# First-layer expert loop of a two-layer diffusion backbone: a third class of experts, four in three units

## The reference, cut to what matters

```python
D_MODEL, SEQ, CTX_LEN, DEPTH = 1024, 256, 256, 2
N_EXPERTS, TOP_K, EXPERT_HIDDEN = 64, 8, 128

def moe_ffn(h, rw, rb, w1, w3, w2, sw1, sw3, sw2):
    scores = jax.nn.sigmoid((h @ rw).astype(F32))
    ...
    _, eidx = lax.top_k(jnp.where(emask, sel, -jnp.inf), TOP_K)
    ...
    a = jnp.einsum('td,edh->teh', h, w1)
    b = jnp.einsum('td,edh->teh', h, w3)
    act = (jax.nn.silu(a) * b * gate[..., None])
    routed = jnp.einsum('teh,ehd->td', act, w2)
    shared = (jax.nn.silu(h @ sw1) * (h @ sw3)) @ sw2
    return (routed + shared)
```

## Time and profile before

| | us |
|---|---|
| median of three runs | 1427.9 (1424.88 to 1430.07) |
| the profiled execution's own time | 1431.2 |
| its span | 1429.1, mean granted clock 0.953 |
| TensorE (PE) busy | 1285.2 (90% of the span) |
| its weight loads (PEld) | 705.7 |
| VectorE (DVE) busy | 544.0 (38%) |
| ScalarE (ACT) busy | 293.5 (21%) |
| GpSimd (POOL) busy | 301.1 (21%) |
| DMA | 373.30 MB, mean 261 GB/s |
| chain that ended last | PE 41%, SyncE's queue 12%, DMA 8%, DVE 4% |

### The profile page before, as it was taken

How to read it: one execution, slowest core, us unless ns; L and a number is a source line. 1 busy time by engine, 2 the same in 40 slices (tenths; PEclk the granted TensorE clock), 3 DMA queues, 4 the chain that set the end, 5 groups by cost and what they waited for, 6 DMA issues and landing times.

```text
span 1429.1 us, 19065 instructions
## 1 busy us (share of the span) xinstructions
PE 1285.2 (90%) x6356; PEld 705.7 (49%) x6357; DVE 544.0 (38%) x1327; ACT 293.5 (21%) x715; POOL 301.1 (21%) x394
## 2 busy tenths in 40 slices
PE   4999998999968999989898969899987799999993
PEld 1443454444534666655565624475544354545441
DVE  5303533554665222223232207455456521211124
ACT  0100114233111222222221211212611111111110
POOL 1001004334123233333332300101710411111110
PEclk9999999999989999999999989999997899999997
DMA  9875309653355999999999379341322999999960
GB/s 334 328 283 191 142 0 267 238 204 119 140 191 211 332 382 377 363 375 370 383 378 390 119 299 364 125 155 25 94 104 83 399 397 392 404 408 398 404 250 31
DMA packets 113083, 373.30 MB, mean 261 GB/s; under 512 B 17978, under 2 KB 24380, under 8 KB 104792
## 3 DMA queue, kind: packets, MB, share of 16 engines
q1 hardware_dynamic: 89112, 313.50, 58.4%
q0 software_dynamic: 23008, 55.40, 10.6%
q10 hardware_dynamic: 864, 3.15, 0.6%
HBM read 368.77 MB, written 30.47 MB: 279 GB/s over the span
## 4 chain that ended last, share of the span: by engine, by line
PE 41%; SPq 12%; DMA 8%; DVE 4%; issue 3%; ACT 1%; POOL 0%; POOLq 0%; DVEq 0%; ACTq 0%
PE bank L1335 11%; SPq L647 10%; PE bank L1357 6%; PE bank L1367 5%; PE bank L943 3%; PE bank L1323 3%; DMA qkv<-in_exp_w 2%; PE bank L1145 2%; PE bank L951 2%; DMA weights<-in_exp_w 2%; DMA probs_T<-in_exp_w 2%; PE bank L1036 1%; PE bank L1026 1%; SPq L778 1%; PE bank L1188 1%
## 5 line engine op out<-in xcount | busy, mean ns | idle before, releaser
L1335 PE MATMUL bank<-weights,b_qk 128*64 128x256 f32 (+2 forms) x1040 | 160.8, 386 | 1.8 <-DVE b_qk L2295 1.5
L1335 PEld LDWEIGHTS bank<-weights,b_qk 128*64 128x64 f32 (+2 forms) x1040 | 110.7, 147 | 62.3 <-issue 34.6
L2301 DVE TENSOR_TENSOR expert_act<-silu_a,bank 128x128 f32<-128x128 f32 x76 | 21.9, 288 | 312.6 <-ACT silu_a L1658 312.6
L1367 PE MATMUL bank<-tokens_h,a_k 128*128 128x512 f32 x208 | 103.5, 622 | 0.0
L2532 POOL DMA_INDIRECT shift_scale_gate_norm<-scratch_h,gather_index x82 | 85.1, 1038 | 70.6 <-POOL gather_index L2529 68.4
L1357 PE MATMUL bank<-weights,expert_act_T 128*64 128x512 f32 (+2 forms) x260 | 91.9, 619 | 8.6 <-DMA weights<-in_exp_w 4.1
L1335 PE MATMUL bank<-features_h,b_qk 128*32 128x256 f32 (+2 forms) x512 | 95.2, 381 | 0.4
L1323 PE MATMUL bank<-tab,shift_scale_gate_norm 128*128 128x128 f32 x624 | 83.0, 276 | 8.4 <-DMA shift_scale_gate_norm<-scratch_h,gather_index 8.4
L1145 PE MATMUL bank<-weights,features_h 128*128 128x512 f32 x192 | 85.9, 602 | 1.3 <-ACT features_h L1445 0.7
L1658 ACT ACTIVATE silu_a<-bank 128x128 f32<-128x128 f32 x76 | 21.1, 278 | 314.7 <-PE bank L1335 314.7
L1323 PEld LDWEIGHTS bank<-tab,shift_scale_gate_norm 128*128 128x128 f32 x624 | 75.9, 191 | 17.6 <-issue 16.9
(11 more groups left out here) (360 smaller groups left out, 1960.4 us busy)
## 6 DMA issues: line engine op xcount, KB each, us to landing
weights<-in_exp_w SPq DMA_DIRECT2D x195, 512.0 KB, 12.1
features_h<-in_exp_w SPq DMA_DIRECT2D x64, 512.0 KB, 11.1
qkv<-in_exp_w SPq DMA_DIRECT2D x64, 512.0 KB, 15.8
shift_scale_gate_norm<-in_ada_w SPq DMA_DIRECT2D x24, 1024.0 KB, 8.8
a_q<-in_exp_w SPq DMA_DIRECT2D x32, 512.0 KB, 13.1
weights<-in_w_in SPq DMA_DIRECT2D x6, 2048.0 KB
shift_scale_gate_norm<-scratch_mod POOLq DMA_DIRECT2D x16, 512.0 KB, 8.7
c_padded<-in_ada_w SPq DMA_DIRECT2D x8, 1024.0 KB, 6.0
```

The costliest lines, as they stand in the source:

```text
L1335: mm = pe.matmul(ab[r, 0:2 * HIDDEN].rearrange("p (m h) -> p m h", m=2), XGT[:, u.slot() % 2, k, r], expert_w13(slot)[:, :, k, :], start=k ...
L1367: mm = pe.matmul(ACC[g][h][:, :], GROW[:, u.slot() % 2, g * P:(g + 1) * P], YSB[:, u.slot() % 2, h * HALF:(h + 1) * HALF], start=False, st ...
```

## The change

The classes become a table. In the first layer, the 24 experts of ranks 30 to 53 get 96 slot rows each instead of a unit of 128 each; four of them fill three units. The last ten experts keep a unit each. A middle expert of such a group has its 96 rows as strips of 64 and 32, which may lie in different units, so its weights are used by two units. Six groups make 18 units where there were 24, so the first layer has 44 units instead of 50, and `BLOCKS` there is 79 instead of 85. A group's three units run directly after one another. A load into a ring slot waits for the last unit that uses the expert that was there. The second layer keeps its units; its routing arithmetic is now written in the general form. `SHARE` of the first layer, the rows in which slots are counted, becomes 32.

```diff
@@ -46,12 +46,25 @@
 TILES = 4
 STREAMS = ((0, 1), (2, 3))
 FULL = ((0, 1, 2, 3), (2, 3))
-QUADS = (0, 8)
-PAIRS = (15, 14)
-SINGLES = tuple(EXPERTS - 4 * q - 2 * p for q, p in zip(QUADS, PAIRS))
-UNITS = tuple(q + p + f for q, p, f in zip(QUADS, PAIRS, SINGLES))
+QUAD = (tuple((e, slice(32 * e, 32 * e + 32)) for e in range(4)),)
+PAIR = (tuple((e, slice(64 * e, 64 * e + 64)) for e in range(2)),)
+FOUR_IN_THREE = (((0, slice(0, 64)), (0, slice(64, 96)), (1, slice(96, 128))),
+                 ((1, slice(0, 64)), (2, slice(64, 128))),
+                 ((2, slice(0, 32)), (3, slice(32, 64)), (3, slice(64, 128))))
+SINGLE = (((0, slice(0, P)),),)
+CLASSES = (((15, PAIR, 2), (6, FOUR_IN_THREE, 3), (10, SINGLE, 4)),
+           ((8, QUAD, 1), (14, PAIR, 2), (4, SINGLE, 4)))
+
+
+def experts_of(shape):
+
+    return 1 + max(e for unit in shape for e, _ in unit)
+
+
+UNITS = tuple(sum(n * len(shape) for n, shape, _ in classes) for classes in CLASSES)
+BOUNDS = tuple((c[0][0] * experts_of(c[0][1]), c[0][0] * experts_of(c[0][1]) + c[1][0] * experts_of(c[1][1])) for c in CLASSES)
 ALWAYS = (1, 0)
-SHARE = (64, 32)
+SHARE = (32, 32)
 UNROLL = 4
 RING = 3
 MASKED = -1e30
@@ -84,22 +97,27 @@
 
 def sequence(l):
 
-    held = SINGLES[l] - UNROLL if l < DEPTH - 1 else SINGLES[l]
-    kinds = [[QUADS[l], 4, 0, 0], [PAIRS[l], 2, QUADS[l], 4 * QUADS[l]],
-             [held, 1, QUADS[l] + PAIRS[l], 4 * QUADS[l] + 2 * PAIRS[l]]]
-    every, order = sum(k[0] for k in kinds), []
+    classes, held = CLASSES[l], UNROLL if l < DEPTH - 1 else 0
+    many = [n for n, _, _ in classes]
+    many[2] -= held
+    every, order = sum(many), []
     for n in range(every):
-        late = [((n + 1) * k[0] / every - order.count(i), i) for i, k in enumerate(kinds)]
...
+        late = [((n + 1) * k / every - order.count(i), i) for i, k in enumerate(many)]
         order.append(max(late)[1])
-    order += [2] * (SINGLES[l] - held)
-    seq, x, done = [], 0, [0, 0, 0]
+    order += [2] * held
+    column = [0, classes[0][0] * len(classes[0][1])]
+    column.append(column[1] + classes[1][0] * len(classes[1][1]))
+    where = [0, *BOUNDS[l]]
+    seq, x = [], 0
     for i in order:
-        _, many, column, where = kinds[i]
-        seq.append((column + done[i], [(x + j, where + many * done[i] + j) for j in range(many)]))
-        done[i] += 1
-        x += many
+        shape = classes[i][1]
+        for unit in shape:
+            seq.append((column[i], [(x + e, where[i] + e, r) for e, r in unit]))
+            column[i] += 1
+        x += experts_of(shape)
+        where[i] += experts_of(shape)
     for n in range(ALWAYS[l]):
-        seq.append((UNITS[l] + n, [(x + n, EXPERTS + n)]))
+        seq.append((UNITS[l] + n, [(x + n, EXPERTS + n, slice(0, P))]))
     return seq
...
-STRIPS = {n: tuple(slice(i * P // n, (i + 1) * P // n) for i in range(n)) for n in (1, 2, 4)}
...
 
                 def products(u, experts):
 
-                    rows = STRIPS[len(experts)]
-                    for slot, fills in experts:
+                    for slot, fills, _ in experts:
                         pe.wait_ge(L[f"w13_in{slot}"], fills * 32)
                     pe.wait_ge(L["xT_scalar"], u.n(1))
                     pe.wait_ge(L["xT_vector"], u.n(1))
                     for k in range(KD):
-                        for (slot, _), r in zip(experts, rows):
+                        for slot, _, r in experts:
                             mm = pe.matmul(ab[r, 0:2 * HIDDEN].rearrange("p (m h) -> p m h", m=2),
                                            XGT[:, u.slot() % 2, k, r], expert_w13(slot)[:, :, k, :],
...
-                    rows = STRIPS[len(experts)]
                     if h == 0:
                         pe.wait_ge(L["actT"], u.n(1))
...
-                    for (slot, _), r in zip(experts, rows):
+                    for slot, _, r in experts:
                         mm = pe.matmul(yp[h][r, :], ACTT[:, r], expert_w2(slot)[:, h * HALF:(h + 1) * HALF],
                                        start=True, stop=True)
                     mm.then_inc(L["y_ps"], 1)
...
-                    was, experts = (experts if n else None), [(x % ring_n, x // ring_n + 1) for x, _ in listed]
+                    was, experts = (experts if n else None), [(x % ring_n, x // ring_n + 1, r) for x, _, r in listed]
                     products(u, experts)
...
-                two, four = 4 * QUADS[l], 4 * QUADS[l] + 2 * PAIRS[l]
+                one, (two, four) = CLASSES[l][0][2], BOUNDS[l]
+                more_two, more_four = CLASSES[l][1][2] - one, CLASSES[l][2][2] - CLASSES[l][1][2]
                 count, key, rank, cap, base, over, upto, t0, t1, t2, t3 = (NB1[0:EXPERTS, i:i + 1] for i in range(11))
                 b = filled(("count", l))
                 iota = const("iota_slot")[0:EXPERTS, 0:EXPERTS]
@@ -2171,18 +2187,15 @@
                 dve.wait_ge(vector_step, steps[0])
                 link(ts(key, count, float(EXPERTS), const("iota_expert")[0:EXPERTS, :], ALU.mult, ALU.subtract))
                 link(stt(RT[0:EXPERTS, 7, 128:128 + EXPERTS], KEY, key, ALL1, ALU.is_lt, ALU.mult, accum_out=rank))
-                if QUADS[l]:
-                    free(ts(t0, rank, two - 0.5, 1.0, ALU.is_gt, ALU.add))
-                    free(ts(t1, rank, four - 0.5, 2.0, ALU.is_gt, ALU.mult))
-                    free(ts(t2, rank, -float(two), 0.0, ALU.add, ALU.max))
-                    link(ts(t3, rank, -float(four), 0.0, ALU.add, ALU.max))
-                    free(tt(cap, t0, t1, ALU.add))
-                    link(stt(base, t3, 2.0, t2, ALU.mult, ALU.add))
-                    link(tt(base, base, rank, ALU.add))
-                else:
-                    free(ts(cap, rank, four - 0.5, 1.0, ALU.is_gt, ALU.add))
-                    link(ts(t0, rank, -float(four), 0.0, ALU.add, ALU.max))
-                    link(tt(base, t0, rank, ALU.add))
+                free(ts(t0, rank, two - 0.5, float(more_two), ALU.is_gt, ALU.mult))
+                free(ts(t1, rank, four - 0.5, float(more_four), ALU.is_gt, ALU.mult))
+                free(ts(t2, rank, -float(two), 0.0, ALU.add, ALU.max))
+                link(ts(t3, rank, -float(four), 0.0, ALU.add, ALU.max))
+                free(stt(cap, t0, float(one), t1, ALU.add, ALU.add))
+                free(ts(base, rank, float(one), None, ALU.mult))
+                link(ts(t2, t2, float(more_two), None, ALU.mult))
+                link(stt(t3, t3, float(more_four), t2, ALU.mult, ALU.add))
+                link(tt(base, base, t3, ALU.add))
                 link(stt(t2, cap, -float(SHARE[l]), count, ALU.mult, ALU.add))
                 link(ts(over, t2, 0.5, None, ALU.is_gt))
...
                 link(tt(t1, upto, over, ALU.subtract))
                 link(ts(t1, t1, float(P // SHARE[l]), float(P // SHARE[l] * UNITS[l]), ALU.mult, ALU.add))
-                link(tt(t1, t1, t3, ALU.subtract))
...
+                free(tt(R(1)[:, EXPERTS:2 * EXPERTS], R(1)[:, EXPERTS:2 * EXPERTS], R(1)[:, 0:EXPERTS], ALU.subtract))
```

More of the change, by code:

```diff
@@ L763, in _ @@
                 every, ring_n = len(SEQUENCE[l]), RING_X
-                where = {x: w for _, experts in SEQUENCE[l] for x, w in experts}
-                user = {x: n for n, (_, experts) in enumerate(SEQUENCE[l]) for x, _ in experts}
+                where = {x: w for _, experts in SEQUENCE[l] for x, w, _ in experts}
+                user = {x: n for n, (_, experts) in enumerate(SEQUENCE[l]) for x, _, _ in experts}
                 def load_w13(slot, n, gone=None):
@@ L1406, in _ @@
                             slot, fills = c - every, i + (-(-(EXPERTS + ALWAYS[l] - (c - every)) // ring_n) + 1)
-                            products(u, [(slot, fills)])
+                            products(u, [(slot, fills, slice(0, P))])
                             act_T(u)
                             tokens_T(At(i, c + 1))
-                            second(u, [(slot, fills)], 0)
-                            second(u, [(slot, fills)], 1)
+                            second(u, [(slot, fills, slice(0, P))], 0)
+                            second(u, [(slot, fills, slice(0, P))], 1)
                             if summed:
```

## The result

The changed kernel takes 1451.59 us, median of four runs (1448.92 to 1453.57), beside 1426.84 us for the kernel before (the three runs shown above and a fourth, 1425.78): a ratio of 1.0166, 95% interval 1.0145 to 1.0188. It is slower by 1.7%, clear of the spread of the runs. The profiled execution of the change is its fastest run, 1448.92 us, span 1447.0; that of before lies above all its timed runs, 1431.2, span 1429.1. So the two profiles stand 17.9 us apart where the medians stand 24.7. The stretch between the two loops, where only the second layer's routing arithmetic is changed, took 308.8 us in the one profile and 305.4 in the other (306.8 to 309.1 in the other kernels of this study), and the change's execution was 2.5 us ahead before its router's chain.

A forecast was written before the change was run, and what follows sets the result against it. It took the busiest DMA engine as bound, TensorE close under it. Base 298 and mixed widths 84 put the loop's end 23.3 us later; with routing +0.2 that made 1454.7, as a median 1451.4 us; range 1440 to 1490.

The forecast's parts named there:

- one engine's count: First layer's loop: rows of the busiest DMA engine, 0.160 us each, account for 350 of 355 us.
- Mixed units: First layer's 12 units with 64- and 32-column strips: widths exclude each other, +7.0 us a unit, +84 us.
- Fewer units: First layer's loop: 24 singles become 18 units, leaving 11 singles and 33 strip units; TensorE base 298 us.
- Less load on the busiest engine: First layer's gathers and scatters: 331 rows instead of 384, 17.0 us earlier, worth nothing where TensorE is the bound.
- Slots: Weight ring: a strip pair first frees two slots at once; with DMA no bound, 0.
- extra blocks: Expert with 139 rows exceeds its share by 11; the always-run unit takes them, extra loop stays empty: 0.
- gate steps: VectorE's gate steps in units 26 to 41, now of 44; VectorE is busy 5 of 20 us: 0.
- Routing: Both layers' routing arithmetic: VectorE's longer chain +0.9 us, fewer one-hot columns about -0.7, together +0.2.
- The first: First layer's loop: unequal strips overlap, TensorE needs 298 us, busiest DMA engine binds; 1409.5 us; chance 0.34.
- The second, total bytes: First layer's loop: unequal strips overlap, but total bytes bind, not one engine; 0 to -4, 1425 us; chance 0.06.
- Overflow: First layer's classes: if ranks or bases were off, extra turns of four units, over 26 us each; 1480; 0.03 with another rival.
- A slow last DMA engine: Last engine, usually slower, gets 177 rows instead of 81: +31 us if it bound, 1459; 0.03 with another rival.

The follow-up runs named there:

- evened: Kernel before, with the rows of 17 of its 34 single units in the first layer moved by 64 partitions: 1419.7 us, ratio 0.9926.
- dealt out inside them: Kernel before, with only the slots of each block of 32 spread four partitions apart: 1420.06 us, ratio 0.9932.
- equal strips: The change with every 64-column strip of a mixed-width unit split into two of 32: 1409.28 us, ratio to the kernel before 0.9866.
- width by width: The change with all k steps of a mixed-width unit's 64-column strip before those of its 32-column strips: 1431.77 us, ratio to the kernel before 1.0017.
- the mixed singles: Kernel before's classes and 50 units, 12 one-expert units computed as strips of 64, 32 and 32, spread among the others: 1499.45 us, ratio 1.0514.
- their control: Kernel before's classes and 50 units, the same 12 one-expert units computed as four strips of 32, spread among the others: 1430.98 us, ratio 1.0010.
- the change dealt out: The change, mixed widths kept, with the slots of each block of 32 spread four partitions apart: 1446.76 us, ratio to the kernel before 1.0126.
- equal strips dealt out: The change with 64-column strips of mixed-width units split into 32s and slots of each 32-block spread four partitions apart: 1395.86 us, ratio to the kernel before 0.9785.
- the run with pairs last: Equal strips dealt out, with the four units held to the first loop's end being pairs instead of singles: 1388.38 us, ratio to the kernel before 0.9712.

## Why the prediction was right, point by point

*What bounded the kernel before.* TensorE close under the loads, as read. That the loads were held back by uneven DMA engines was right, and the halves were the main part of it (evened: 13.1 us of the first loop; dealt out inside them: 3.6). That one engine's count gives the time was too simple: it overrates rows inside a half. And layer 1, whose 409 GB/s served as the full rate, was not without room itself: its loop lost 5.5 to 6.1 us by dealing out alone, which no term had.

*Mixed units.* The mechanism was right and decided the sign. Strips of two widths run one after the other: equal strips, width by width, and the mixed singles with their control each show it. The term was a little small: products of 9.02 and 8.49 us are 5.4 and 4.9 above those with equal strips (5.0 forecast), since a change costs 0.13 us and not 0.10, and the halves take 1.99 and 1.94 where equal ones take 1.01. By whole units it is 7.2 us, not 7.0, and 86 in all. These rows agree with the Trainium skill's sentence that a change of tiling mode drains TensorE (TensorEngine Tiling (Array Packing), Key Properties). What the Trainium skill says of the overlap of tiles in different column groups (TensorE: Matmul & The Clock Gate, Part 3) holds here for equal widths only; the zero price that it would have given failed by those 86 us of TensorE time.

*Fewer units.* The base of 298 us was too high. The loop of the change less its 12 x 7.2 is 294.9, that is 6.70 us for each of 44 units: with equal strips a strip unit takes 6.6 to 6.8 us from products to products, while 6.92 was the price of a pair between singles with both changes of width. This error of 3 us and that of the mixed units, 2.4 us the other way, cancelled: 382.0 us of loop forecast, 381.3 measured. The 1451.4 so came out closer than its parts deserve.

*Less load on the busiest engine*: nothing where TensorE binds. Shown: the change dealt out has the same loop, 381.2.

*Slots, extra blocks, gate steps*: no wait of TensorE on any of them in the first loop. *Routing*: +0.4 in the chain and -1.3 in the one-hots, where +0.9 and -0.7 were priced. That gain of 0.9 us didn't reach the loop, which began 1.9 us earlier after a lead of 2.5. Behind the one-hots TensorE has its products of L1188 (now L1205) to finish, 9.6 us of them now where 8.1 were left before. So in this trace the routing cost 0.6 us, not 0.2.

*Rivals.* The first was the right account of the kernel once the widths are equal, to 0.2 us in time; since its count of rows turned out too simple and its loop 3.4 us too long, part of that is luck. The second, total bytes, was wrong for the kernel before. It fits once the rows are spread in both ways, as in equal strips dealt out (by the counts, halves of 2179 and 1917 rows): 408 to 411 GB/s in every stretch from 520 to 760 us. Overflow did not occur. A slow last DMA engine showed nowhere: at 410 GB/s the mean share of the sixteen is 1.03, as in the earlier trace rows, which leaves little idle time for any of them.

What stays open: whether the 0.13 us of a change is a drain, or the load of the next strip's weights that nothing covers; both would look so. The runs also don't tell whether the rows of a half are held up in the DMA engines or at the partitions that they read and write, as moving rows by 64 partitions changes both; and the 8 us of the mixed singles beyond their loop's price stay unexplained.

## What to carry to other kernels

Pack strips of one width into a unit, even when that means more matmuls: four strips of 32 cost the same as one of 128 (3.6 us of products), but a 64 beside two 32s costs twice that when each width runs in one piece (7.15 us), and two and a half times when they alternate (9.02). Here six units fewer saved 36 us of TensorE's time, and the mixed widths took 86. Where rows of a gather or scatter may be absent, count them by the DMA engine that serves their partitions, first by halves of 64; the sum of the bytes doesn't show it. And when a change moves the bound to another engine, first take away that engine's new cost: here two lines of a table turned +1.7% into -1.3%.

## What was not expected of the hardware

A strip of 64 columns alone, or two of 32 side by side, takes as long for the 16 instructions of a strip (3.58 us) as all 128 columns (3.53 to 3.65). The second layer's loop, at 392 to 408 GB/s on the page before, still had 2% to give to a better spread of its gathered rows (272.7 us of loop, dealt out 266.8). And TensorE at full clock without a single hole was a sign of the slower kernel: mean clock 0.966 in the change, 0.953 before, 0.950 in the run with pairs last.
